# The chunked recurrence's inverse with its two tiles half a level apart, and the second tile's products in one run

## What is computed

```python
def step(S, inp):
    r_t, w_t, k_t, v_t, a_t, b_t = inp
    sa = jnp.einsum('bhvk,bhk->bhv', S, a_t)
    S = S * w_t[:, :, None, :] + sa[..., None] * b_t[:, :, None, :] + v_t[..., None] * k_t[:, :, None, :]
    y = jnp.einsum('bhvk,bhk->bhv', S, r_t)
    return S, y
...
gates = jax.nn.sigmoid(p_gate.astype(jnp.float32)).reshape(bsz, t, N_BRANCHES, D_MODEL)
merged = (gates[:, :, 0] * (y_a @ w_proj_a[l]) + gates[:, :, 1] * (y_b @ w_proj_b[l])
          + gates[:, :, 2] * (y_c @ w_proj_c[l]))
```

## Time and profile before

| | |
|---|---|
| median of 3 runs | 1547.15 us |
| profiled execution | 1547.55 us |
| its span | 1545.8 us |
| PE busy | 1521.3 us (98%) |
| DVE busy | 1074.6 us (70%) |
| ACT busy | 415.7 us (27%) |
| recurrence, first to last level | about 354 to 571 us of the span |

### The profile page before, as it was taken

The page is one execution under the profiler, slowest core; times in us unless marked ns, Lnnn a source line. Parts: engine busy times, 40 slices in busy tenths (PEclk is TensorE's granted clock), DMA queues, the critical chain, the costliest instruction groups (busy, mean ns, idle before and its releaser), DMA issues.

```text
span 1545.8 us, 23866 instructions
## 1 busy us (share of the span) xinstructions
PE 1521.3 (98%) x9310; PEld 1098.0 (71%) x9310; DVE 1074.6 (70%) x2049; ACT 415.7 (27%) x791; POOL 131.6 (9%) x107
## 2 busy tenths in 40 slices
PE   9999999999999999999999999999999999999997
PEld 7885544457777777676545674587858888888886
DVE  5975857885556546687698993658678887785553
ACT  3345274531111113101465664103010000000001
POOL 0020020032002100000197000000000000000000
PEclk9999999999999999999999999999999999999999
DMA  7122111121111112322122221220222222223321
GB/s 281 68 81 82 55 51 54 49 67 57 43 57 57 57 47 98 123 96 82 61 76 82 68 83 66 85 82 28 74 80 91 84 82 82 85 97 92 91 86 69
DMA packets 48720, 121.62 MB, mean 79 GB/s; under 512 B 5408, under 2 KB 19488, under 8 KB 48352
## 3 DMA queue, kind: packets, MB, share of 16 engines
q1 hardware_dynamic: 47088, 115.89, 22.3%
q10 hardware_dynamic: 1296, 2.89, 0.5%
q0 software_dynamic: 224, 1.31, 0.2%
HBM read 117.98 MB, written 2.10 MB: 78 GB/s over the span
## 4 chain that ended last, share of the span: by engine, by line
PE 84%; DVE 13%; ACT 1%; issue 1%; DMA 0%; DVEq 0%; SPq 0%; ACTq 0%
PE bank L650 16%; PE bank L796 6%; PE opair L1455 4%; PE vpair L1455 4%; PE bank L1455 3%; PE apair L1455 3%; PE vpair L680 3%; PE opair L680 3%; PE opair L1484 2%; PE vpair L1484 2%; DVE arena L2076 2%; DVE arena L2085 2%; PE vpair L730 2%; PE apair L680 2%; DVE arena L2834 2%; PE apair L1484 2%
## 5 line engine op out<-in xcount | busy, mean ns | idle before, releaser
L650 PE MATMUL bank<-h,ring 128*128 128x512 f32 x560 | 254.1, 596 | 0.8 <-ACTq L1618 0.8
L650 PEld LDWEIGHTS bank<-h,ring 128*128 128x128 f32 x560 | 102.8, 190 | 115.7 <-issue 111.4
L2076 DVE TENSOR_TENSOR arena<-ring 128x512 f32<-128x512 f32 (+2 forms) x148 | 91.1, 615 | 73.3 <-DMA ring<-weights 48.1
L650 PE MATMUL bank<-arena,ring 128*128 128x512 f32 (+1 forms) x320 | 119.3, 515 | 2.0 <-ACT arena L1622 1.9
L2085 DVE SCALAR_TENSOR_TENSOR arena<-arena,cols 128x512 f32<-128x512 f32 (+1 forms) x129 | 94.9, 735 | 4.6
L650 PEld LDWEIGHTS bank<-arena,ring 128*128 128x128 f32 x320 | 57.9, 190 | 47.0 <-issue 40.3
L3117 POOL TENSOR_TENSOR arena<-arena 128x512 f32<-128x512 f32 x47 | 61.6, 1310 | 10.4 <-ACT arena L1930 6.9
L2076 DVE TENSOR_TENSOR arena<-arena 128x256 f32<-128x256 f32 (+1 forms) x114 | 57.6, 505 | 6.0 <-PE bank L1007 2.1
L3122 POOL TENSOR_TENSOR h<-h,sq 128x512 f32<-128x512 f32 x2 | 2.5, 1266 | 695.2 <-ACT sq L2040 695.1
L2020 ACT ACTIVATE arena<-arena 128x512 f32<-128x512 f32 x22 | 13.9, 630 | 127.7 <-DVE arena L2085 127.6
L2076 DVE TENSOR_TENSOR arena<-arena,ring 128x512 f32<-128x512 f32 (+2 forms) x74 | 45.0, 609 | 3.7 <-DVE arena L2076 0.6
(11 more groups left out here) (401 smaller groups left out, 3147.4 us busy)
## 6 DMA issues: line engine op xcount, KB each, us to landing
ring<-weights SPq DMA_DIRECT2D x169, 512.0 KB, 3.7
ring<-weights SPq DMA_DIRECT2D x36, 256.0 KB, 3.0
ring<-weights SPq DMA_DIRECT2D x68, 128.0 KB, 2.4
x<-xt SPq DMA_DIRECT2D x8, 512.0 KB, 8.4
ring<-weights SPq DMA_DIRECT2D x40, 64.0 KB, 2.0
cst<-cst_in ACTq DMA_DIRECT2D x1, 1056.0 KB, 7.6
arena<-memt SPq DMA_DIRECT2D x2, 512.0 KB, 6.3
arena<-mem2t POOLq DMA_DIRECT2D x1, 1024.0 KB, 5.0
```

The source lines that it names most:

```text
L650: last = mm(o[:, 0:n], weight(), src, start=c == 0, stop=c == len(srcs) - 1)
L2076: do(V.tensor_tensor(out, a, b, op), sig)
```

## The change

On PE the function of one level is split in two, `new_left(l, tiles)` and `new_right(kind, l, i)`, the second for one tile and one product. Level 1 still makes both lefts at once (with `keys_by_values` behind them), but only the first tile's rights. From level 2 on a level is one run: left of the first tile, the two rights that the second tile still owes from the level before, left of the second tile, the two rights of the first; behind it come, in levels 2 and 3, the transposes, and then all 8 pairs of filling. The second tile's last right goes in front of `rk_gram`, and `weighted` follows without filling. In the second tile's part the 4 pairs in front of the state step go behind `weighted`, which makes 8. DVE and ACT take the pieces in the new order. `O_BEFORE` counts uses of `opair` for a later stage. The filling is the same in number and order, and so is the arithmetic.

```diff
+                def new_left(l, tiles):
+                    rows = CROSSED[l - 1]
                     o = take_pair("v")
-                    for i in range(2):
+                    for i in tiles:
                         pe.wait_ge(ml_ready.sem, 10 * p + 2 * (l - 1) + i + 1)
...
+                def new_right(kind, l, i):
...
+                    o = take_pair(kind)
+                    pe.wait_ge(y_ready.sem, 10 * p + 2 * (l - 1) + i + 1)
+                    pe.wait_ge(xt_ready.sem, 12 * p + 2 * (l - 1) + i + 1)
...
+                rb_gram(t0)
+                new_left(1, (0, 1))
+                keys_by_values(t0)
+                fill(work, 4)
+                new_right("a", 1, 0)
+                new_right("o", 1, 0)
+                fill(work, 4)
+                for l in range(2, 6):
+                    new_left(l, (0,))
+                    new_right("a", l - 1, 1)
+                    new_right("o", l - 1, 1)
+                    new_left(l, (1,))
                     if l < 5:
...
+                        new_right("a", l, 0)
+                    new_right("o", l, 0)
                     if l in (2, 3):
                         transposed(t0, bb if l == 2 else k)
+                    fill(work, 8)
+                new_right("o", 5, 1)
+                rk_gram(t0)
                 weighted(t0)
                 fill(work, 4)
...
                 rb_gram(t1)
                 keys_by_values(t1)
-                fill(work, 4)
                 state_products(2 * t0 + 1)
                 rk_gram(t1)
                 weighted(t1)
-                fill(work, 4)
+                fill(work, 8)
...
+            def new_xx(p, i):
+                o = a_pair()
+                do(fn(XX_[p][i], heads_of(o[:, :, 4 * i * C:4 * (i + 1) * C]), ACT.Copy), xx_next)
+                a_read_inc(2)
...
+                for l in range(2, 6):
+                    new_xx(p, 1)
                     if l < 5:
...
+                        new_xx(p, 0)
                     if l in (2, 3):
                         token_rows(bT if l == 2 else kT)
                     read_through(reading, GATED, u0 + 8 + 4 * l)
...
+                for l in range(2, 6):
+                    take_left(p, (0,))
+                    take_right(p, 1)
                     read_through(reading, GATED, u0 + 4 + 4 * l)
...
+                    take_left(p, (1,))
+                    take_right(p, 0)
                     next_sums(1)
                     read_through(reading, GATED, u0 + 6 + 4 * l)
...
                     next_sums(1)
+                take_right(p, 1)
+                take_rk(t0)
...
                 take_rb()
+                take_states(2 * t0 + 1)
+                take_rk(t1)
                 next_sums(2)
                 read_through(reading, GATED, u0 + 36)
```

More of the change, by code:

```diff
@@ L573, in build @@
         P_BEFORE = 8 + 16
-        O_BEFORE = P_BEFORE + (2 * 5 + 2 * (2 + 2 + 2) + 2) * (NT // 2)
+        O_BEFORE = P_BEFORE + (2 * 2 * 5 + 2 * (2 + 2 + 2) + 2) * (NT // 2)
         KK_AT = 8
@@ L1250, in _ @@
                             pe.wait_ge(xx_next.sem, 8 * p + 2 * (l - 2) + i + 1)
-                        last = quad_products(o, rows, head(ML_[i]), head(XX_[p][i], xx_kind), None, rows, slot_=i)
+                        xx = head(XX_[p][i], CROSSED[l - 2] if l > 1 else "b")
+                        last = quad_products(o, rows, head(ML_[i]), xx, None, rows, slot_=i)
                     for ins in last:
                         v_done.inc(ins)
-                    fill(work, 4)
-                    if l < 5:
[L1256 to L1271, removed]
@@ L1272, in _ @@
-                    fill(work, 4)
+                def new_right(kind, l, i):
+                    rows, turned = CROSSED[l - 1], TURNED[l - 1]
+                    yt = head(YT_[p][i], rows)
+                    old = head(XT_[p][i], TURNED[l - 2] if l > 1 else "b")
+                    o = take_pair(kind)
+                    pe.wait_ge(y_ready.sem, 10 * p + 2 * (l - 1) + i + 1)
+                    pe.wait_ge(xt_ready.sem, 12 * p + 2 * (l - 1) + i + 1)
+                    if kind == "a":
+                        for ins in quad_products(o, rows, old, yt, rows, None, slot_=i):
+                            a_done.inc(ins)
+                    else:
+                        for ins in quad_products(o, turned, yt, old, rows, CROSSED[l], slot_=i):
+                            o_done.inc(ins)
@@ L1854, in _ @@
                 read_through(reading, GATED, u0 + 8)
-                for l in range(1, 6):
-                    if l == 2:
-                        weighted_values()
+                weighted_values()
+                new_xx(p, 0)
+                read_through(reading, GATED, u0 + 12)
+                for l in range(2, 6):
+                    new_xx(p, 1)
                     if l < 5:
[L1859 to L1862, removed]
+                        new_xx(p, 0)
                     if l in (2, 3):
@@ L1872, in _ @@
                 weighted_values()
-                read_through(reading, GATED, u0 + 36)
                 weights_out()
@@ L2580, in take_inverse_grams, with take_left, take_right @@
                 tt(XT, masked, mask_by_bank("ident64"), ADD, xt_ready)
+            def take_left(p, tiles):
+                o = v_pair()
+                for i in tiles:
+                    tt(YT_[p][i], chunk_product(o, i), mask_by_bank("ident64"), ADD, y_ready)
+                signal_now(v_read)
+                signal_now(v_read)
+            def take_right(p, i):
+                o = o_pair()
+                copy(XT_[p][i], chunk_product(o, i), xt_ready)
+                signal_now(o_read)
+                signal_now(o_read)
             def take_rb():
@@ L2641, in _ @@
                 take_inverse_grams(p, 1)
-                for l in range(1, 6):
-                    read_through(reading, GATED, u0 + 4 + 4 * l)
[L2644 to L2650, removed]
+                read_through(reading, GATED, u0 + 8)
+                take_left(p, (0, 1))
+                take_rb()
+                next_sums(1)
+                read_through(reading, GATED, u0 + 10)
+                take_right(p, 0)
+                next_sums(1)
+                for l in range(2, 6):
+                    take_left(p, (0,))
+                    take_right(p, 1)
+                    read_through(reading, GATED, u0 + 4 + 4 * l)
+                    take_left(p, (1,))
+                    take_right(p, 0)
                     next_sums(1)
                     read_through(reading, GATED, u0 + 6 + 4 * l)
[L2653 to L2659, removed]
                     next_sums(1)
+                take_right(p, 1)
+                take_rk(t0)
                 read_through(reading, GATED, u0 + 28)
```

2 lines of the change are left out of this document (removed).

## The result

The changed kernel takes 1551.61 us (median of 7 runs, 1551.27 to 1552.35), the kernel before beside it 1547.30: a ratio of 1.0028, 95% interval 1.0018 to 1.0038. It is slower, by 4.3 us. The forecast was 1550.5, with a range of 1547.4 to 1554.0. The profiled execution after has a span of 1549.9 us against 1545.8, 4.1 more.

What follows compares the result with a forecast made beforehand. PE, busy 98% of the span, was taken as the bound. Terms -3.3 + 4.9 + 1.7 + 0.1 = +3.4 us, added to the median 1547.15, gave 1550.5 us; range 1547.4 to 1554.0.

Steps and rivals of the forecast that it cites:

- Second left: Levels 2 to 5: PE waits for ACT's copy of the second tile's new `XX`, 0.61 us each, +4.9 us in two passes.
- Transposes: Levels 2 and 3: transposes behind the first tile's rights wait for ACT to copy product `a`, 0.43 us four times, +1.7 us.
- Runs saved: Fewer seams between small products and filling in levels, weighted products and second tile's part: 1.63 us a pass, -3.3 us.
- Other waits in the runs: Remaining PE waits within runs: only level 5's first-tile `o`, waiting for DVE's copy out of `opair`, 0.05 us, +0.1 both passes.
- Copies that stay hidden: Rival: PE's blocks behind `a` cover ACT's path, so only the seams count, 1543.9 us; chance 0.08.
- DVE late at the gate banks: Rival: in filling, PE waits some 0.5 us for DVE in each of 8 sets, +4, 1554.5 us; chance 0.10.

Runs made afterwards that it cites:

- the half copy: Changed kernel with ACT copying only two of four head columns of the second tile's new `XX`, the rest left out: 1550.51 us, ratio 1.0020.
- the filling between with DVE in order: Changed kernel with 4 filling pairs between the second tile's rights and left, transposes behind the other 4, DVE's reading reordered to match: 1548.42 us, ratio 1.0009.
- the last kernel: Kernel with one run a level (rights, then next lefts), two filling pairs moved from behind its second run to in front: 1550.84 us, ratio 1.0025.

## Why the prediction was right

The forecast was slower by 3.4 us of span, and 4.1 came, by the steps foretold.

- **Second left, +4.9.** The start of the second left was put at 1.99 behind the run's start; it came at 2.00, 2.06 at level 4:

```profile
387.48 0.69 PE L1119 MATMUL vpair<-arena 64*64 64x64 f32 x32
...
389.54 0.69 PE L1119 MATMUL vpair<-sq,arena 64*64 64x64 f32 x32 [0.44 <-ACT sq L1865]
...
398.18 0.69 PE L1119 MATMUL vpair<-arena 64*64 64x64 f32 x32
```

  This level, without transposes, takes 10.70 us (forecast 10.66; 10.40 before). ACT started 0.09 behind `a`'s end rather than 0.16 (at level 4 it was 0.16, hence the 2.06), and PE followed 0.14 behind the copy rather than 0.06: two small errors that cancel, which was luck. The head paid again was 0.03 (0.49 to the next start) and not 0.06. The size held, and the half copy and the filling between with DVE in order showed the cause.
- **Transposes, +1.7.** Put at 3.98, they came at 3.95. The runs with them amid the filling took this term away alone, 1.5 us.
- **Runs saved, -3.3.** From the grams of r and b to the first outputs, the first pass takes 59.29 us before (353.80 to 413.09) and 61.63 after (353.59 to 415.22), 2.3 more. The waits add 2.4 + 0.8 + 0.4 there (second left, transposes, and the two mis-sized below), so 1.3 was saved, as forecast (3 x 0.35 + 0.23); this is a difference, not a measurement by itself. The second tile's part, from its A V block to its outputs, fell by 0.34 and 0.25 us (0.35 forecast), with no wait in its run.
- **Mis-sized: "Other waits in the runs".** The `o` of the first tile at level 5 was to wait 0.05 us; its row starts 0.68 behind the second left where 0.49 is usual, so some 0.2: DVE's copy ended at 2.48, as foreseen (2.50), but PE followed 0.21 behind it and not 0.06. And the filling of 4 pairs behind the joined weighted products takes 1.96 + 1.91 us instead of 1.83 + 1.81, since it stands in front of gate banks that DVE has not yet read (0.4 of the waits of weight loads in the list, once in each pass). I had counted nothing there.

```profile
400.19 0.69 PE L1119 MATMUL vpair<-sq,arena 64*64 64x64 f32 x32 [0.37 <-ACT sq L1865]
400.87 0.69 PE L1119 MATMUL opair<-arena 64*64 64x64 f32 x32
...
411.35 1.99 PE L796 MATMUL bank<-h,arena 128*128 128x256 f32 x8
413.31 1.98 PE L650 MATMUL bank<-arena,ring 128*128 128x512 f32 x4
```

  Together 0.4 us a pass, of which 0.05 had been forecast: with two passes, about the 0.7 us by which the sum fell short.
- **The rivals.** Copies that stay hidden: the eight waits refute it. DVE late at the gate banks in each of 8 sets: its waits are 1.4 us in four, on the weight loads alone, and 0.7 us in two stood there before; the two new ones are those behind the joined weighted products. The mechanism is there, at under a fifth of the price (0.7 of 4 us). It struck fully (2.5 us at once) only where DVE's stream was out of PE's order.

The Trainium skill, TensorEngine Tiling (Array Packing), section Performance Considerations (PSUM Bottleneck), says that the copy out of PSUM may become the limit of packed products. This case agrees once nothing covers the copy: with a block at 0.46 and a copy at 0.60 the run waited in all eight places, and with half the copy it waited 0.21 less in each.

## What to carry to other kernels

Before joining two short runs, lay out from the starts of the blocks when the copy that the next block needs can end, with the lag on both sides; a run saved was worth some 0.3 us here, one uncovered copy cost 0.6. Moving a wait is no gain unless the engine that serves it has cover in the new place too, and whoever reorders the producer must reorder every engine that reads its banks. Only the joins that need no fresh copy cost nothing here; what they win, 0.65 us, the times do not separate from no change.

## What was not expected of the hardware

- A run of 192 of these small matmul instructions, each with its weight load, stalled with no releaser at a fixed count of instructions: PE stood for 0.7 to 1.0 us in a run that takes 3.3 us elsewhere, and for 2.2 us where 512 KB of weights were in transit ahead of an instruction packet. In all six stalls PE went on 1.24 to 1.32 us behind such a packet's end, as if it had outrun its instructions. Of eight such runs in an execution two stalled; why these two, no run shows. The Trainium skill, Runtime: NRT & Kernel Launch, section Instruction fetch mechanics, says that instructions come in blocks of 256, and that their coming is mostly hidden. The stall's place, fixed by a count, is in keeping with the first, though no run here shows the number 256; the second failed in these runs, if the packet was PE's.
- Behind idle stretches of 2.48 and 2.18 us of PE the granted clock was 0.50 to 0.63 in stretches of 2 us (0.50 is the level of 1.2 GHz), and 8 instructions of filling took 5.40 us (idle time excluded) in one case, against 3.70. A wait of 1.21 us in the last kernel left it at 1.00 in the stretches behind it.
